# Full-height state matmuls and a layer norm moved between convolution columns, in a fused mixer and expert block on one core

## The chip, the cores and the metric

One Trainium2 chip, one of its cores. The core has a matrix engine (TensorE, PE in the profile, with PEld for its weight loads), VectorE (DVE), ScalarE (ACT), GpSimd (POOL), SyncE (SP, which only issues transfers here) and 16 DMA engines. The metric is device microseconds of one execution, lower is better. All tensors are float32 in memory.

## The reference

A transformer-like block on 2048 tokens of width 1024: an adaptive norm, a mixer of two branches, and a mixture of 64 experts. The change touches the mixer only:

```python
h = rms_norm(x, g_pre_mix[l]) * (1.0 + sc_m) + sh_m
z = h @ w_in[l]                                   # z_val | z_gate | z_ssm, 512 columns each
a_out = conv_module(z_val * jax.nn.sigmoid(z_gate), ...)   # depthwise conv of 31 taps, layer norm, silu
b_out = s5_layer(z_ssm, ...)                      # 32 groups: complex state space model, 64 states each
mixed = jnp.concatenate([rms_norm(a_out, g_out_conv[l]), rms_norm(b_out, g_out_ssm[l])], axis=-1)
o = mixed @ w_out[l]
x = x + gt_m * rms_norm(o, g_post_mix[l])

# in s5_layer
bu_r = jnp.einsum('blgh,gph->blgp', uf, bbr)      # and bu_i
_, _, s_r, s_i = lax.associative_scan(_complex_affine_combine, (lam_r, lam_i, bu_r, bu_i), axis=1)
y = (jnp.einsum('blgp,ghp->blgh', s_r, c_re) - jnp.einsum('blgp,ghp->blgh', s_i, c_im) + d_skip * uf)
g = jax.nn.gelu(y)
out = g * jax.nn.sigmoid(g @ w_glu + b_glu)
```

After the mixer come routing (8 of 64 experts for each token), the routed and the shared experts, and a last norm.

## The kernel before, in words

The 2048 tokens are worked through in two halves (`NH` = 2, index `h`) of 1024. A half goes through these stages on PE, in this order in the program:

- `z_ssm(h)`: eight units (`("zs", h, j)`), each 8 matmuls of 128x512, that give u for the state space model; then `u_transposed(h)`, 32 transposes.
- `inputs_to_state(h)`: the input of every chunk of 8 tokens to the states. Four groups `n`, each of two accumulator banks (real and imaginary, `("V", h, n, w)`), from a ring of four banks `dv`, which VectorE frees.
- `z_conv(h)`: 16 units (`("zc", h, q, b, w)`), each 8 matmuls of 128x512, that give value and gate of the convolution branch for channel block `q`; in half 0, transposes of x for half 1 stand between them (`turn_unit`).
- `outputs(h)`: for each of the 32 state groups `g` one accumulation of three matmuls of 128x128: the part inside the chunk (`TOE`, 128 rows high), the real states (`SR`, 64 rows) and the imaginary states (`SI`, 64 rows). A pair of groups shares one tile, one group in the lower and one in the upper 64 partitions. The accumulators (`("Y", h, n)`) are in the ring of two banks `mm`; ScalarE applies the gelu once a pair of banks is full.
- `g_transposed(h)` and `glu(h)`: transposes and the gate matmul.

VectorE runs, for each half, `states(h)` (four groups: phasors, a scan for each of the four pairs and both parts, phasors again) and `conv(h)` (four channel blocks, each one tensor_scalar and 30 scalar_tensor_tensor of 128x1024, accumulated in `cacc`). The layer norm of a half (`norm_turns`, eight token tiles `i`) passes all engines for each tile: PE transposes `cacc` (`("LF", h, i)`), ScalarE copies it to `ytok`, VectorE takes mean and variance (`norm_stats`), GpSimd normalises into `yn`, PE transposes back (`("LB", h, i)`), ScalarE applies gain, bias and sigmoid, GpSimd multiplies and SyncE stores from one of two slots (`bo`). There is one `ytok` and one `yn`. In half 0 the nine turns of this stand between the units of `z_ssm(1)`; in half 1 they follow the end of the GLU and the ada blocks (`ada`, matrix-vector products of the adaptive norm), three of which stand between them. `conv(1)` may overwrite `cacc` only when the last tile of half 0 has been transposed.

Then the output projection begins (`mix_half`), which needs all stored tiles; ScalarE's first square for it (L1411) stands behind its part of the last layer norm turn. Every engine takes its work strictly in the order that the program writes; the numberings `tpk`, `mmk` and `dvk` give the banks of the rings, `sgk` and `bok` the slots of the sigmoid tiles and of the stores. Waits are semaphores.

## Time and profile before

| | us |
|---|---|
| median of the three runs | 3013.49 (3012.6 to 3021.64) |
| the profiled execution, its own time | 3023.36 |
| its span | 3021.6 |
| PE busy | 2710.6 (90%) |
| VectorE busy | 1548.0 (51%) |
| GpSimd busy | 1456.6 (48%) |
| ScalarE busy | 1147.0 (38%) |
| PE's share of the chain that ended last | 61% |
| mixer, up to the first output projection matmul | 796.6 |
| output matmuls, half 0 and half 1 | 54.2 and 55.1 |
| z columns of half 1 | 110.1 |

How to read it: the span is one execution as the hardware profiler saw it. A row of a timeline gives the start, the time from start to end, the engine, the line and operation, what it writes and reads and how many, and in brackets how long the engine was idle before it and which instruction released it. Windows give for a stretch the busy time of each engine (and its instructions), the granted clock of PE as a part of 2.4 GHz, and the share and rate of the DMA engines. A float32 matmul shows as two records, a transpose as one. A busy time is an average over stages with different limits, and the mixer and the experts are limited by different things; the change is in the first quarter of the span.

### The profile page before, as it was taken

How to read it: one execution, taken by the hardware profiler on the slowest of the kernel's cores; microseconds unless marked ns; L12 is line 12 of the kernel's file. 1: busy time of each engine (PE TensorE's matmuls, PEld its weight loads, DVE VectorE, ACT ScalarE, POOL GpSimd, SP SyncE). 2: the span in 40 equal slices, each digit the busy share in tenths (PEclk: the TensorE clock that was granted, in tenths of full speed). 3: DMA queues.
4: the chain of work that ended last, by engine and by line, in shares of the span. 5: the costliest groups of instructions: out<-in, count | busy, mean ns of one | idle time of the engine just before them, and what ended most of it. 6: DMA issues, size and time to landing. Idle time of an engine off the chain costs nothing.

```text
span 3021.6 us, 49743 instructions
## 1 busy us (share of the span) xinstructions
PE 2710.6 (90%) x11527; PEld 1951.1 (65%) x11528; DVE 1548.0 (51%) x2565; ACT 1147.0 (38%) x1537; POOL 1456.6 (48%) x1756
## 2 busy tenths in 40 slices
PE   6989998999678999659999999999999999999980
PEld 2745664462345666548777777777777778777770
DVE  7389918990255666623333333443455444444525
ACT  4133231122322232124444444454555555545532
POOL 2012141112345666424455555555667767767656
PEclk8999699969779999879999999999999999999995
DMA  8152223233422232166777777778889989988977
GB/s 259 59 114 89 102 92 49 84 128 131 161 107 70 99 101 88 50 217 148 191 187 203 215 208 191 189 215 243 239 263 263 269 271 271 268 258 248 268 212 260
DMA packets 306667, 534.90 MB, mean 177 GB/s; under 512 B 40310, under 2 KB 206198, under 8 KB 305834
## 3 DMA queue, kind: packets, MB, share of 16 engines
q1 hardware_dynamic: 252826, 356.19, 35.7%
q0 software_dynamic: 51472, 173.70, 24.3%
q10 hardware_dynamic: 2304, 4.20, 0.4%
q8 instruction: 34, 0.56, 0.1%
q14 instruction: 31, 0.25, 0.0%
HBM read 396.02 MB, written 138.01 MB: 177 GB/s over the span
## 4 chain that ended last, share of the span: by engine, by line
PE 61%; issue 17%; POOL 9%; POOLq 6%; ACT 2%; DVE 2%; SPq 1%; DMA 1%; another core or an unknown queue 0%; ACTq 0%; DVEq 0%
PE psm L1111 27%; PE psm L1058 8%; PE psm L950 7%; PE psm L912 4%; PE psm L1104 2%; PE psm L851 2%; POOL arena L2147 2%; PE psm L988 2%; POOL arena L2144 2%; POOL st L2137 1%; POOLq L2143 1%; PE psm L968 1%; PE psm L967 1%; POOLq L2165 1%; PE psm L1048 1%
## 5 line engine op out<-in xcount | busy, mean ns | idle before, releaser
L1111 PE MATMUL psm<-whi,xhi 128*128 (+1 forms) x1424 | 577.6, 406 | 65.2 <-issue 33.8
L1111 PE MATMUL psm<-whi,xlo 128*128 (+1 forms) x1424 | 559.8, 393 | 0.0
L1111 PE MATMUL psm<-wlo,xhi 128*128 (+1 forms) x1424 | 558.5, 392 | 0.0
L1900 DVE TENSOR_TENSOR arena<-psm,arena 128x256 f32<-128x256 f32 x178 | 75.7, 425 | 653.2 <-ACT arena L1461 645.0
L1111 PEld LDWEIGHTS psm<-whi,xhi 128*128 128x128 f32 x1424 | 269.4, 189 | 139.3 <-issue 67.8
L2152 POOL TENSOR_TENSOR wlo<-raw,whi (+1 forms) x64 | 330.3, 5161 | 42.3 <-ACT whi L1490 42.3
L1111 PE MATMUL psm<-whi,hhi 128*128 (+1 forms) x712 | 295.4, 415 | 41.2 <-issue 19.9
L1739 DVE SCALAR_TENSOR_TENSOR arena<-arena,cw 128x1024 f32<-128x1024 f32 x240 | 326.9, 1362 | 8.6
L1111 PEld LDWEIGHTS psm<-whi,xlo 128*128 128x128 f32 x1424 | 269.5, 189 | 59.2
L2161 POOL DMA_INDIRECT acc_d<-arena x162 | 278.6, 1720 | 58.6 <-issue 54.3
L1111 PEld LDWEIGHTS psm<-wlo,xhi 128*128 128x128 f32 x1424 | 270.4, 190 | 51.7
L1916 DVE TENSOR_TENSOR wlo<-raw,whi (+1 forms) x256 | 296.5, 1220 | 2.8 <-ACT whi L1486 2.8
L1461 ACT ACTIVATE arena<-psm 128x256 f32<-128x256 f32 x178 | 68.4, 384 | 601.8 <-PE psm L1111 594.0
L1111 PE MATMUL psm<-whi,hlo 128*128 (+1 forms) x712 | 282.1, 396 | 0.0
L1111 PE MATMUL psm<-wlo,hhi 128*128 (+1 forms) x712 | 281.2, 395 | 0.0
L1467 ACT COPY arena<-psm 128x1024 f32<-128x1024 f32 x162 | 164.2, 1014 | 224.3 <-PE psm L1111 158.7
L1486 ACT CAST whi<-raw (+1 forms) x256 | 249.4, 1051 | 0.0
L1058 PE MATMUL psm<-arena 128*128 128x512 f32 x512 | 235.6, 620 | 0.0
L1896 DVE TENSOR_TENSOR xlo<-psm,xhi 128x1024 fp32r<-128x1024 f32 x163 | 199.6, 1225 | 66.0 <-ACT xhi L1457 63.5
L950 PE MATMUL psm<-arena 128*128 128x512 f32 x512 | 221.4, 593 | 0.0
L1457 ACT CAST xhi<-psm 128x1024 fp32r<-128x1024 f32 x163 | 165.7, 1017 | 83.7 <-PE psm L1104 83.2
L2147 POOL DMA_INDIRECT arena<-h_d,arena x165 | 179.5, 1088 | 37.1 <-issue 23.9
(354 smaller groups left out, 4024.6 us busy)
## 6 DMA issues: line engine op xcount, KB each, us to landing
raw<-in_we_gate_dram SPq DMA_DIRECT2D x64, 1024.0 KB
raw<-in_we_up_dram SPq DMA_DIRECT2D x64, 1024.0 KB
raw<-in_we_down_dram SPq DMA_DIRECT2D x64, 1024.0 KB
arena<-in_w_ada_dram SPq DMA_DIRECT2D x12, 2048.0 KB
arena<-in_x_dram SPq DMA_DIRECT2D x32, 512.0 KB, 6.0
h_d<-arena SPq DMA_DIRECT2D x17, 512.0 KB, 2.7
acc_d<-arena SPq DMA_DIRECT2D x17, 512.0 KB, 3.6
arena<-in_w_in_dram SPq DMA_DIRECT2D x16, 512.0 KB, 5.5
```

Of the source, the lines that this page charges most:

```text
L950: m = TE.matmul(b[:, :], wz_conv(q)[:, w, k, :], hT[:, k, b2 * 512:(b2 + 1) * 512], start=(k == 0), stop=(k == KD - 1))
L1058: m = TE.matmul(psm[:, 2 * f + c, :], mixb[:, i % 2, f * CT + q, :], wout[:, f * CT + q, c * 512:(c + 1) * 512], start=(q == 0), stop=(q = ...
L1111: m = TE.matmul(o, a, w, start=(n == 0), stop=(n == len(todo) - 1))
L1457: SC.copy(xhi[:, :], psm[:, 2:4, :].rearrange("p a n -> p (a n)")).then_inc(s_xt_high, 1)
L1467: SC.copy(yb[w], psm[:, 4:6, :].rearrange("p a n -> p (a n)")).then_inc(s_y_act, 1)
L1486: SC.copy(whi[:, bass.ds(slot + c * GC, GC)], raw[:, bass.ds(slot + c * GC, GC)]).then_inc(s_whi_ready, 1)
L1739: m = stt(o, v[:, q, k:k + HT], cw[:, q, k:k + 1], o, ALU.mult, ALU.add)
L1896: tt(xlo[:, :], psm[:, 2:4, :].rearrange("p a n -> p (a n)"), xhi[:, :], ALU.subtract).then_inc(s_xt_ready, 1)
L1916: m = tt(wlo[:, bass.ds(slot + c * GC, GC)], raw[:, bass.ds(slot + c * GC, GC)], whi[:, bass.ds(slot + c * GC, GC)], ALU.subtract)
L2147: PO.indirect_dma_start(xg[w], None, h2_d, bass.IndirectOffsetOnAxis(idxg[w], 0)).then_inc([s_xr_in0, s_xr_in1][w], 16)
L2152: PO.tensor_tensor(wlo[:, bass.ds(slot + WG, FE * D)], raw[:, bass.ds(slot + WG, FE * D)], whi[:, bass.ds(slot + WG, FE * D)], ALU.subtrac ...
L2161: PO.indirect_dma_start(acc_d, bass.IndirectOffsetOnAxis(idxs, 0), yb[w], None, compute_op=ALU.add).then_inc(s_ya_out, 16)
```

## The change

The states of a group are no longer in two tiles of 64 rows. `states` writes its last step by halves of the partitions into `SS`, in which real states are in the lower and imaginary states in the upper 64 partitions of each group, so that `outputs` multiplies `SS[:, g]` by one coefficient block `CO[:, g]` of 128 rows: two matmuls for a group, both 128 rows high, instead of three. The coefficients are built from two transposed blocks (`Y1`, `Y2`) with three operations for each of eight powers instead of six on half the width. The accumulators of the outputs come from the ring `dv` of four banks instead of `mm`.

```diff
                 for n in range(8):
-                    b = take_mm(("Y", h, n))
+                    b = take_dv(("Y", h, n))
                     pe.wait_ge(s_states_ready, 4 * h + n // 2 + 1)
                     for j in range(4):
-
-                        g = 8 * (n // 2) + 2 * j + n % 2
-                        r, lo = g // 2, (n % 2) * S
+                        g = 4 * n + j
                         o = b[:, j * P:(j + 1) * P]
                         TE.matmul(o, UT[:, g, :], TOE[:, g, :], start=True, stop=False)
-                        TE.matmul(o, SR[lo:lo + S, r, :], COR[lo:lo + S, r, :], start=False, stop=False)
-                        m = TE.matmul(o, SI[lo:lo + S, r, :], COI[lo:lo + S, r, :], start=False, stop=True)
-                    m.then_inc(s_mm_full, 1)
+                        m = TE.matmul(o, SS[:, g, :], CO[:, g, :], start=False, stop=True)
+                    m.then_inc(s_dv_full, 1)
...
-                    for w, (a, x0, x1, op) in enumerate(((SR, t[0], t[1], ALU.subtract), (SI, t[2], t[3], ALU.add))):
-                        add(tt(a[:, r, 1:NC], x0[:, :, 0:NC - 1], x1[:, :, 0:NC - 1], op))
+                    stacked = both.rearrange("p (r f c) -> p f r c", r=4, f=2)
+                    for w, (x0, x1, op) in enumerate(((t[0], t[1], ALU.subtract), (t[2], t[3], ALU.add))):
+                        for lo, hi, f in halves:
+                            o = stacked[w * S:(w + 1) * S, f]
+                            add(tt(o[:, :, 1:NC], x0[lo:hi, :, 0:NC - 1], x1[lo:hi, :, 0:NC - 1], op))
+                            if h:
+                                add(V.tensor_copy(o[:, :, 0], last[lo:hi, w, r]))
```

The input states of a half are issued in four pieces: groups 0 and 1 ahead of the columns, groups 2 and 3 behind the first and the second column unit. The layer norm of half 0 leaves `z_ssm(1)` and stands behind the first ten column units of half 1, on PE, ScalarE and GpSimd alike; a tile comes back two turns after it went out instead of one, and `ytok`, `yn` and `bn` are double.

```diff
             def z_conv(h):
                 units = list(UNITS) if h == 0 else []
...
+                for n in range(2):
+                    input_state(h, n)
+                for u, (q, b2, w) in enumerate(ZC_UNITS):
...
+                    if u < 2:
+                        input_state(h, u + 2)
...
+                    if h == 1 and u < TPH + 2:
+                        norm_turn(0, u)
...
+            def norm_turn(h, i):
+                if i == 0:
+                    pe.wait_ge(s_conv_ready, CT * (h + 1))
+                if i < TPH:
+                    b = take_tp(("LF", h, i))
+                    for q in range(CT):
+                        m = TE.transpose(b[:, q * P:(q + 1) * P], cacc[:, q, i * P:(i + 1) * P], ident[:, :])
+                    m.then_inc(s_tp_full, 1)
+                if i >= 2:
+                    b = take_tp(("LB", h, i - 2))
+                    pe.wait_ge(s_yn_ready, h * TPH + i - 1)
+                    for q in range(CT):
+                        m = TE.transpose(b[:, q * P:(q + 1) * P], yns[h][i % 2][:, q * P:(q + 1) * P], ident[:, :])
+                    m.then_inc(s_tp_full, 1)
```

On VectorE the statistics of half 0's tiles are placed inside `states(1)`; on SyncE the stores of these tiles come between the table and weight loads of half 1:

```diff
+                    if h and n >= 2:
+                        norm_stats(2 * n - 3)
...
+                    if h and 1 <= n <= 3:
+                        norm_stats(2 * n - 2)
+                if h:
+                    for k in range(5, TPH):
+                        norm_stats(k)
...
-            for i in range(TPH):
+            for i in range(2):
                 store_bo(("ln", 0, i))
             load_toe(1)
             load_wz_conv(1, 2)
+            for i in range(2, 6):
+                store_bo(("ln", 0, i))
             load_wz_conv(1, 3)
+            for i in range(6, TPH):
+                store_bo(("ln", 0, i))
```

How this stands on PE, from the end of half 0's GLU to the outputs of half 1. Before: L912 is z_ssm, L1002 and L1008 are the two transposes of a layer norm turn, L923 transposes u, L938 is the input states, L950 the columns.

```order
L912 MATMUL psm<-arena 128x512 x8
L1002 MATMUL psm<-ident,arena 128x128 x4
L1008 MATMUL psm<-ident,arena 128x128 x8
L923 MATMUL psm<-ident,arena 128x128 x32
L938 MATMUL psm<-arena 64x128 x64
L950 MATMUL psm<-arena 128x512 x128
```

And of the changed kernel, where L915 is z_ssm, L926 transposes u, L941 is the input states, L954 the columns, L1003 and L1009 the two transposes of a turn:

```order
L915 MATMUL psm<-arena 128x512 x64
L926 MATMUL psm<-ident,arena 128x128 x32
L941 MATMUL psm<-arena 64x128 x32
L954 MATMUL psm<-arena 128x512 x8
L941 MATMUL psm<-arena 64x128 x16
L1003 MATMUL psm<-ident,arena 128x128 x4
L954 MATMUL psm<-arena 128x512 x8
L941 MATMUL psm<-arena 64x128 x16
L1003 MATMUL psm<-ident,arena 128x128 x4
L954 MATMUL psm<-arena 128x512 x8
L1003 MATMUL psm<-ident,arena 128x128 x4
L1009 MATMUL psm<-ident,arena 128x128 x4
```

The eight units of z_ssm now stand in one piece, the last two input-state groups stand behind a column unit each, and the turns of the layer norm begin behind the first column unit.

On VectorE, the third of the four state groups of half 1 (L1717 is its scans, L1722 and L1723 its second phasor products, L1729 and L1731 the stacked writes and their first columns, L1737 the signal to PE, L1690 the statistics of a tile):

```order
L1717 SCALAR_TENSOR_TENSOR arena<-lam,last,arena 128x128 x8
L1690 BN_STATS bn<-arena 128x6
L1691 BN_AGGR bn<-bn 128x2
L1722 TENSOR_TENSOR arena<-arena 128x512 x2
L1723 TENSOR_TENSOR arena<-arena 128x512 x2
L1729 TENSOR_TENSOR arena<-arena 64x4x127
L1731 COPY arena<-last 64x4
L1729 TENSOR_TENSOR arena<-arena 64x4x127
```

Before, the same place held two writes of 128 partitions instead of four of 64, and the eight statistics stood in a row ahead of the first group. Now the first statistics stand behind the second group, and the last three between the fourth group and the convolution.

## Rows read from the trace of the kernel before

**Rows 1.** Windows of the mixer's stages: us, busy us of each engine, clock, DMA:
```profile
151.00:157.50 6.50, 4.60 (x33) 3.37 (x32) 0.00 (x0) 4.88 (x10) 0.00 (x0) 1.00 0.85 230
...
157.50:174.00 16.50, 8.67 (x128) 8.29 (x128) 14.84 (x33) 8.56 (x13) 3.54 (x8) 0.79 0.16 38
...
292.40:346.60 54.20, 52.14 (x194) 39.58 (x192) 52.73 (x42) 5.94 (x9) 1.39 (x3) 0.60 0.23 88
346.60:357.00 10.40, 7.96 (x33) 5.86 (x32) 10.11 (x9) 9.28 (x11) 0.00 (x0) 0.50 0.56 205
357.00:386.70 29.70, 29.67 (x64) 13.19 (x65) 19.93 (x14) 6.09 (x8) 12.70 (x21) 0.93 0.37 123
386.70:463.10 76.40, 70.11 (x225) 51.94 (x223) 7.71 (x22) 30.17 (x65) 35.49 (x51) 0.96 0.27 90
...
480.40:590.50 110.10, 110.10 (x258) 48.90 (x257) 107.41 (x119) 8.87 (x15) 12.06 (x21) 1.00 0.31 48
...
655.60:683.30 27.70, 27.68 (x65) 12.10 (x66) 27.13 (x17) 6.07 (x8) 12.88 (x21) 1.00 0.70 247
...
683.30:722.80 39.50, 39.50 (x92) 6.69 (x91) 0.39 (x1) 11.18 (x13) 2.38 (x5) 1.00 0.65 225
...
722.80:793.20 70.40, 37.65 (x119) 13.32 (x119) 10.77 (x22) 24.72 (x53) 33.72 (x46) 0.72 0.36 128
```

**Rows 2.** Timeline of PE, input states of half 0 (start, us, line, records, idle before):
```profile
157.56 5.46 PE L938 MATMUL psm<-arena 128*64 128x128 f32 x96 [0.67 <-ACT arena L1311]
...
170.79 3.32 PE L938 MATMUL psm<-arena 128*64 128x128 f32 x32 [7.77 <-DVE arena L1705]
```

**Rows 3.** Timeline of PE, output matmuls of half 0:
```profile
292.42 0.39 PE L967 MATMUL psm<-arena 128*128 128x128 f32 x2
...
292.74 0.48 PE L968 MATMUL psm<-arena 64*128 64x128 f32 x2
...
313.28 0.79 PE L967 MATMUL psm<-arena 128*128 128x128 f32 x2
...
315.91 0.80 PE L967 MATMUL psm<-arena 128*128 128x128 f32 x2 [0.69 <-ACT arena L1342]
```

**Rows 4.** Windows: transposes of x; one us in the outputs of each half:
```profile
67.00:76.00 9.00, 7.59 (x46) 4.90 (x44) 8.76 (x22) 8.31 (x13) 0.00 (x0) 0.96 0.10 41
...
303.00:304.00 1.00, 1.00 (x6) 0.77 (x5) 1.00 (x1) 0.00 (x0) 0.00 (x0) 0.65 0.99 410
...
600.00:601.00 1.00, 1.00 (x6) 0.80 (x4) 0.96 (x2) 0.11 (x1) 0.00 (x0) 0.63 1.03 422
```

**Rows 5.** Timeline of VectorE: convolution of half 0, states, convolution, layer norm:
```profile
377.21 0.18 DVE L1746 COPY arena<-arena 128x30 f32<-128x30 f32 x1
...
475.51 0.67 DVE L1704 TENSOR_TENSOR arena<-psm,arena 128x512 f32<-128x512 f32 x1
...
486.63 0.67 DVE L1704 TENSOR_TENSOR arena<-psm,arena 128x512 f32<-128x512 f32 x1
...
510.83 0.81 DVE L1737 TENSOR_SCALAR arena<-arena,cw,col 128x1024 f32<-128x1024 f32 x1
...
724.10 0.69 DVE L1754 BATCH_NORM_STATS2 bn<-ytok 128x6 f32<-128x512 f32 x1 [40.41 <-ACT ytok L1372]
```

**Rows 6.** Timeline of GpSimd, normalising a tile:
```profile
726.09 2.09 POOL L2069 TENSOR_SCALAR arena<-ytok,bn,st 128x512 f32<-128x512 f32 x1
```

**Rows 7.** Timeline of SyncE, table loads of half 1:
```profile
480.56 9.37 SPq L610 DMA_DIRECT2D arena<-kd_d  x8
```

**Rows 8.** Timeline of PE, first turn of the last layer norm, next ada block:
```profile
728.33 1.09 PE L1008 MATMUL psm<-ident,arena 128*128 128x128 f32 x4 [4.45 <-POOL arena L2069]
...
729.35 9.02 PE L851 MATMUL psm<-arena,ccol 128*1 128x512 f32 x16
```

**Rows 9.** Timelines of SyncE and GpSimd, last tiles of the last layer norm:
```profile
774.51 19.49 SPq L619 DMA_DIRECT2D mix_d<-bo  x5
...
783.56 1.26 POOL L2058 TENSOR_TENSOR bo<-ly,arena 128x512 f32<-128x512 f32 x1 [11.33 <-DMA mix_d<-bo]
```

More of the change, by code:

```diff
@@ L357, in build @@
         UNIT_STEPS = (3, 3, 2, 0, 2, 2, 2, 2)
+        ZC_UNITS = [(q, b, w) for q in range(CT) for b in range(2) for w in range(2)]
         tpk = []
@@ L889, in tables @@
                 pe.wait_ge(s_c_ready, 1)
-                for w in range(3):
+                for w in range(2):
                     b = take_dv(("C", w))
@@ new lines, in z_conv @@
+                for u, (q, b2, w) in enumerate(ZC_UNITS):
+                    if b2 == 0 and w == 0:
+                        pe.wait_ge([s_wz_in0, s_wz_in1][q % 2], (80, 64)[q % 2] * h + 32 * (q // 2 + 1))
+                    b = take_mm(("zc", h, q, b2, w))
+                    for k in range(KD):
+                        m = TE.matmul(b[:, :], wz_conv(q)[:, w, k, :], hT[:, k, b2 * 512:(b2 + 1) * 512],
+                                      start=(k == 0), stop=(k == KD - 1))
+                    m.then_inc(s_mm_full, 1)
+                    if u < 2:
+                        input_state(h, u + 2)
+                    if h == 0 and w == 1:
+                        for n in range(UNIT_STEPS[2 * q + b2]):
+                            turn_unit(1, *units.pop(0))
+                    if h == 1 and u < TPH + 2:
+                        norm_turn(0, u)
@@ L1029, in _ @@
                 ada(n)
-            norm_turns(1)
+            for i in range(TPH + 2):
+                norm_turn(1, i)
+                if 1 <= i <= 3:
+                    ada(8 + i)
             pe.wait_ge(s_mm_free, len(mmk))
@@ L1403, in _ @@
                 ada(n)
-            norm_turns(1)
+            for i in range(TPH + 2):
+                norm_turn(1, i)
+                if 1 <= i <= 3:
+                    ada(8 + i)
             def square_mix(i):
@@ L1702, in states @@
                     r = slice(4 * n, 4 * n + 4)
+                    both = us[:, n * 1024:(n + 1) * 1024]
+                    SR, SI = (both[:, w * 512:(w + 1) * 512].rearrange("p (r c) -> p r c", r=4) for w in range(2))
                     vr = got(("V", h, n, 0)).rearrange("p (r c) -> p r c", r=4)
@@ L2025, in gate @@
             def gate(h):
-                for q in range(CT):
-                    for b in range(2):
+                for u, (q, b, w) in enumerate(ZC_UNITS):
+                    if w == 1:
                         pool.wait_ge(s_mm_free, MMN["zc", h, q, b, 1] + 1)
@@ L2035, in gate @@
                             row_stats(3)
+                    if h == 1 and u < TPH + 2:
+                        norm_turn(0, u)
             def out_slot(key):
@@ L2088, in _ @@
             PO.memset(st[:, 61:62], 0.0).then_inc(s_zero_ok, 1)
-            norm(1)
+            for i in range(TPH + 2):
+                norm_turn(1, i)
             pool.wait_ge(s_row_ready, 1)
```

281 lines of the change are left out of this document (114 added, 167 removed).

## The prediction

> **What bounds the kernel now.** I read the windows by stage first, to see which engine is full where; then the timelines at the seams between stages, where an engine waits; then the way from the last layer norm into the output projection, since that is where every microsecond won before it has to arrive. The matrix engine (PE) sets the pace of the mixer. In the windows it is busy nearly all the time in the z columns (110.1 of 110.1 us), in the output matmuls (52.1 of 54.2 us in half 0) and in the GLU [rows 1], so what it no longer does there comes off. Three places are slow for other reasons. The input-state stage of half 0 takes 16.5 us for work that PE does in about 7: it waits 7.77 us for VectorE to give back accumulators, and runs the last quarter at the low clock [rows 1, 2]. The output matmuls start at 0.32 us each (292.42 to 292.74) and end at 0.65 each (three of them between 313.28 and the 0.69 us gap before 315.91) [rows 3]: the granted clock falls from 1.00 to 0.50, that is from 2.4 to 1.2 GHz, in the window 303 to 304, and its mean over the stage is 0.60 [rows 1, 4]. And half 0's layer norm stands between z_ssm of half 1 and the next stage, 76.4 us for all of it, the transposes of u included [rows 1].
>
> VectorE is the other engine that matters. The convolution of half 1 begins at 510.83; four channel blocks later, at 683.7, VectorE goes idle for 40.41 us, until PE has come to the last layer norm at 722.8 [rows 5]. So the convolution of half 1 has 39 us of slack behind PE. This slack decides what the change is worth.
>
> **The change, part by part**, on the profiled execution (span 3021.6 us, 3023.4 us with what lies around it; that is 0.3% above the median of the runs, 3013.5, so I take the difference from it and set it on the median).
>
> (a) Input states among the columns. PE does the first 96 records of this stage in 5.46 us [rows 2], so all 128 take 7.3; the third and fourth group of banks now come behind a column unit of 6.9 us each (110.1 / 16, rows 1), by when VectorE has freed the banks (it reads a group's two banks in the first four of its operations, at 0.67 us each, and needs 11.1 us for the group, rows 5). 16.5 - 7.3 = **9.2 us** off PE in half 0.
>
> (b) Output matmuls. 64 in a half instead of 96. At 0.32 us [rows 3] they take 20.5, at 0.65 us 41.6. A full-height one costs what a half-height one costs: the first row of the pair at 292.42 is full height, and the next starts 0.32 us after it. I take 20.5, since I expect the clock to stay up, for two reasons in the rows: the two thirds of matmuls that used 64 of 128 rows are gone, and the gap of 0.69 us, two banks waiting for ScalarE, goes with the ring of four banks; in both halves it fell, in the windows 303 to 304 and 600 to 601 [rows 4], a little after the first such gap, 10 to 11 us into the stage. In the stage of transposes of x from 67 to 76 us PE had more idle time than the outputs will have (7.59 of 9.0 us busy) and kept a clock of 0.96 over it, all full height [rows 4]. So 54.2 - 20.5 = **33.7 us** off half 0. If it falls after 11 us as before, 34 are done by then and 30 x 0.65 = 19.5 follow: 30.5 in all, 23.7 off.
>
> The Trainium skill, "TensorE: Matmul & The Clock Gate", section "Why this matters for your kernels", ties the loss of the fast clock to idle gaps between bursts of matmuls; by that alone the outputs would not have fallen at all, with one gap of 0.69 us, and the measured row decides against it. By the page the sum is as it stands, by the row taken alone (the outputs fell while busy, so they fall again) it is 12 us less.
>
> (c) What follows the outputs in half 0 starts at full clock: transposes 10.4 to 9.3 us (eight ScalarE copies of about 1.0 set them), GLU 29.7 to the 27.7 that half 1 has at clock 1.00 [rows 1]. **3.1 us**.
>
> (d) Layer norm of half 0 leaves the z_ssm stage. Left are eight units of 7.0 and the transposes of u, 6.5 [rows 1]: 62.7 instead of 76.4, **13.7 us**.
>
> (a) to (d) bring the input states of half 1 from 463.1 to 463.1 - 59.7 = 403.4. VectorE ends the convolution of half 0 at 377.4 before [rows 5]; its four state groups of half 0 grow by 1.3 us each, so near 382 now, and it is free by then.
>
> (e) The z columns of half 1 carry the layer norm. PE's own work: 7.3 + 110.1 + 16 x 0.44 for transposes = 124.5. But turn i asks for the normalised tile of turn i - 2, and that passes VectorE (statistics placed inside the state groups: the first only after two groups), GpSimd and ScalarE, each in order. Walking the turns through all four engines, with VectorE's group at 11.1 us [rows 5] plus 2 x 0.61 for two more stacked writes and 0.2 for copies, lengthened to 13.2 for contention, and a GpSimd pass of 3.8 (2.09 for the normalising itself [rows 6], 1.1 for the two small steps and hand-overs ahead of it, from 725.0 to 726.09, and the rest for contention), PE waits 9 us in turns 4 to 6 and does the last unit at +134. The eighth tile leaves for VectorE at +77, its copy and statistics take 1.7, and only then may the convolution overwrite its accumulator: it starts at **+79** (before: +47.7). With nothing stretched it is +76, with 15% more +83. So 403.4 + 79 = 482.4 instead of 510.8, and at the same 172.9 us its end is **655.3**. PE is there at 403.4 + 134 + 20.5 + 9.3 + 27.7 + 39.5 (five ada blocks [rows 1]) = 634.4. It waits 21 us. All that half 1's outputs save, 55.1 - 20.5 = 34.6 us, is inside this wait, and so is a weight load that now queues behind the table load (9.4 us of issue [rows 7]), which may hold PE up to 10 us at column unit 8.
>
> (f) The last layer norm starts at 655.3 instead of 722.8: **67.5 us**. It no longer waits 4.45 us for the first tile [rows 8]; against it PE comes out of the long wait at the low clock, and pays 2 us as the first ada block did before (9.02 instead of 7.0) [rows 8]. Two transposes in a row come first: 2.3 us gained. Behind the last ada block SyncE's queue sets the pace as before: the modulation is stored, the row constants are loaded, then the fourth tile is stored at 774.5, and GpSimd, which needs its slot, goes on at 783.56 [rows 9]. Then three steps instead of four, about 2 us gained. Together **4 us**, between 0 and 6.
>
> VectorE's table of output coefficients is three 512-wide operations a step instead of six 256-wide: about 2 us less, in a stretch where it is idle afterwards. Nothing for it, nor for the third coefficient transpose, behind which PE waited for ScalarE anyway. The experts stage is untouched; I take 0, within 5 either way.
>
> Sum: 67.5 + 4 = 71.5 us. 3023.4 - 71.5 = 2951.9 for the profiled run; on the median, 3013.5 - 71.5 = **2942 us**.
>
> **Rivals.**
> 1. The clock falls in the outputs all the same (for it: PE is 96% busy there and it fell; against: full height, no gap). Half 0 then gives 12 us less ((b) 10, (c) 2 to 3), and half 1's loss disappears in the wait: 2954. One variant: the Trainium skill's same page, section "Part 4: PE-mode transpose", says that transposes don't count as activity for the clock. By that only (c) would go, 2945, with a chance of 0.04 inside the forecast's range. The rows speak against it: the clock stood at 0.96 over 9 us in which PE did nothing but transposes [rows 4].
> 2. The turns of the layer norm hold each other up more than in my walk: GpSimd's products stretch while VectorE works (state groups now coincide with them). Each 5 us later at the eighth tile is 5 us on the end, to +95: 2945 to 2958.
> 3. Slower than before: the turns don't overlap at all. One turn is then a unit 6.9, transposes 0.9, copy 0.6, statistics 1.0, GpSimd 3.8 + 2.0 + 1.9 for normalising, product and gate, ScalarE 2.2 and a store of 2 that holds the output slot: 21 us, eight of them 168. The convolution starts at +172, ends at 748, and the total is 3013 + 25 - 4 = 3034. It decides from a turn of 18 us on; between 8 and 10 are in the walk, so it takes a double.
> 4. The 4 us of (f) or the experts stage move by another phase of the queues: 2936 to 2950. In the forecast's range.
>
> **How the numbers follow.** Forecast 0.60 (2935 to 2949), rival 1 0.24, rival 2 0.11, slower 0.02, other 0.03. The range 2929 to 2961 takes in the forecast, rival 1 with its spread, and most of rival 2. About 0.3% is what a measurement of this kernel can tell from no change, 9 us: no case but the serial one comes near it. Faster 0.96, same 0.02, slower 0.02.
>
> **What would show it.** After: no idle of VectorE's making in the input states of half 0; output stages near 21 us with clock 1.00 (rival 1: 30, mean near 0.7); input states of half 1 at 403; first convolution step of half 1 at 482, 79 us later; an idle time of PE near 21 us before the last layer norm, released by VectorE, where before VectorE idled 40; the first output-projection matmul at 722. The forecast is wrong if PE doesn't wait for the convolution there: then half 1's outputs count, and the sum of (e) is the step that failed.

## The result and the profile after

The changed kernel takes 2939.64 us (median of 4 runs, 2926.55 to 2954.06), the kernel before 3015.78 in the same comparison (4 runs, 3012.6 to 3021.64): a ratio of 0.976, 95% interval 0.972 to 0.980. The profiled execution took 2938.84 us, its span is 2937.1. Forecast were 2942 us, between 2929 and 2961. Against the 3015.78 us of the same comparison the gain is 76.1 us, where 71.5 were forecast; the four runs of the changed kernel lie 27.5 us apart, so the total alone can't test a sum of terms of a few microseconds. The marks below can.

The times that follow are marks in the mixer, read as starts of instructions on PE. From the start of the program to the input states of half 0 all kernels here but the one before have the same code, and yet that mark lies anywhere from 154.7 to 159.0 us; so the columns behind the first count from it. Even from there to the input states of half 1 the same code takes 238.6 to 240.3 us (six kernels), so a difference of marks under 2 us between two runs says nothing. Each experiment was executed once, but for the last two (six times); the mixer is read from one profiled execution each.

| kernel | input states of half 0 | to those of half 1 | to the last layer norm | from there to the output projection | mark to output projection | rest of the span |
|---|---|---|---|---|---|---|
| before | 157.6 | 305.5 | 565.2 | 73.8 | 639.0 | 2225.0 |
| after | 155.0 | 239.3 | 494.1 | 74.8 | 568.9 | 2213.3 |

The mixer gave 70.2 us from that mark on (72.8 with the 2.6 us ahead of it). The rest of the span, where the code is the same, was 11.7 us shorter; over the ten profiled runs of the changed kernel and of its variants with the same output that part lies between 2194 and 2220 us, so 12 us are within what it varies by, and I take them for no effect of the change.

PE's windows after, by stage: input states and the first two column units of half 0; outputs, transposes of g and GLU of half 0; z columns of half 1; outputs of half 1; five ada blocks (columns as in [rows 1]):

```profile
154.90:176.60 21.70, 21.61 (x161) 12.88 (x161) 19.82 (x42) 11.06 (x16) 4.70 (x9) 1.00 0.12 29
281.10:295.40 14.30, 14.30 (x130) 14.30 (x129) 13.94 (x12) 5.94 (x9) 2.30 (x3) 1.00 0.75 284
295.40:305.10 9.70, 6.16 (x34) 4.22 (x32) 9.45 (x8) 9.17 (x11) 0.00 (x0) 0.82 0.78 290
305.10:332.70 27.60, 27.58 (x65) 12.40 (x66) 26.99 (x18) 6.08 (x8) 14.93 (x21) 1.00 0.39 133
394.30:538.60 144.30, 128.94 (x448) 63.20 (x449) 125.44 (x170) 29.90 (x63) 55.16 (x69) 0.95 0.31 51
538.60:553.00 14.40, 14.40 (x130) 14.39 (x129) 14.04 (x11) 5.14 (x8) 2.27 (x3) 1.00 0.81 292
589.60:629.20 39.60, 39.57 (x91) 6.69 (x90) 38.60 (x30) 11.18 (x13) 2.46 (x7) 1.00 0.65 225
```

The outputs take 14.3 and 14.4 us in the two halves at clock 1.00, where [rows 1] has 54.2 at 0.60. The next rows are PE's timeline: the input states, now 3.71 and twice 1.97 us with no wait for VectorE (against 7.77 us in [rows 2]), a wait for a weight load at the ninth column unit of half 1, the wait for the convolution, and the output projection.

```profile
154.99 3.71 PE L941 MATMUL psm<-arena 128*64 128x128 f32 x64 [0.68 <-ACT arena L1306]
165.70 1.97 PE L941 MATMUL psm<-arena 128*64 128x128 f32 x32
174.66 1.97 PE L941 MATMUL psm<-arena 128*64 128x128 f32 x32
...
481.14 1.22 PE L954 MATMUL psm<-arena 128*128 128x512 f32 x1 [9.81 <-DMA arena<-in_w_in_dram]
...
649.07 1.97 PE L1003 MATMUL psm<-ident,arena 128*128 128x128 f32 x8 [19.90 <-DVE arena L1754]
...
720.44 3.54 PE L1046 MATMUL psm<-one,arena 128*128 128x1 f32 x16 [21.34 <-ACT arena L1403]
723.84 2.06 PE L1056 MATMUL psm<-arena 128*128 128x512 f32 x2
```

Before the last layer norm it is now PE that waits, 19.90 us, for the last operation of the convolution (L1754), where VectorE waited 40.41 [rows 5]. VectorE's timeline: it is done with the convolution of half 0 at 382, waits 12.71 us for half 1's input states, then idles in the layer norm's last statistics before the convolution of half 1 (L1752) starts at 472.42.

```profile
382.06 0.42 DVE L1698 TENSOR_TENSOR arena<-lam,last 128x16 f32<-128x16 f32 x4
395.49 0.69 DVE L1706 TENSOR_TENSOR arena<-psm,arena 128x512 f32<-128x512 f32 x1 [12.71 <-PE psm L941]
...
464.53 0.69 DVE L1690 BATCH_NORM_STATS2 bn<-ytok 128x6 f32<-128x512 f32 x1 [7.35 <-ACT ytok L1366]
471.60 0.69 DVE L1690 BATCH_NORM_STATS2 bn<-arena 128x6 f32<-128x512 f32 x1 [6.15 <-ACT arena L1366]
472.42 0.80 DVE L1752 TENSOR_SCALAR arena<-arena,cw,col 128x1024 f32<-128x1024 f32 x1
```

### The profile page after: what moved, and what is told of

Read it like the earlier page. It is cut to its first block, busy times and chain, and to the rows that moved or that the text cites. A ratio compares the mean times of both kernels' runs of the same rounds, so it can differ in the third digit from the quotient of the medians.

```text
span 2937.1 us, 49464 instructions
## 1 busy us (share of the span) xinstructions
PE 2620.7 (89%) x11395; PEld 1888.8 (64%) x11396; DVE 1571.1 (53%) x2558; ACT 1145.9 (39%) x1534; POOL 1471.7 (50%) x1756
## 4 chain that ended last, share of the span: by engine, by line
PE 51%; issue 19%; POOL 11%; DVE 9%; POOLq 7%; ACT 2%; DMA 1%; SPq 1%; DVEq 0%; ACTq 0%
PE psm L1109 25%; PE psm L1056 8%; DVE arena L1754 6%; PE psm L954 5%; PE psm L915 4%; POOL arena L2149 3%; POOL arena L2146 2%; PE psm L1102 2%; POOL st L2139 2%; POOLq L2145 2%; POOLq L2167 2%; PE psm L854 1%; PE psm L1046 1%; POOLq L2166 1%; POOLq L2158 1%
## 5 line engine op out<-in xcount | busy, mean ns | idle before, releaser
L1754 DVE SCALAR_TENSOR_TENSOR arena<-arena,cw 128x1024 f32<-128x1024 f32 x240 | 335.7, 1399 | 8.6
L954 PE MATMUL psm<-arena 128*128 128x512 f32 x512 | 226.5, 600 | 9.8 <-DMA arena<-in_w_in_dram 9.8
L1911 DVE TENSOR_TENSOR hlo<-psm,hhi 128x256 fp32r<-128x256 f32 x178 | 74.9, 421 | 230.0 <-ACT hhi L1471 228.1
```

The source lines that it names most:

```text
L954: m = TE.matmul(b[:, :], wz_conv(q)[:, w, k, :], hT[:, k, b2 * 512:(b2 + 1) * 512], start=(k == 0), stop=(k == KD - 1))
L1754: m = stt(o, v[:, q, k:k + HT], cw[:, q, k:k + 1], o, ALU.mult, ALU.add)
```

## Experiments

A line in a diff is against the changed kernel. Where a kernel's output differs, the experts stage routes other tokens, so only the mixer is read there. "Relative" means against the mark of the input states of half 0.

### What the output matmuls cost, and what let the clock fall

**Two 64-row matmuls for the second one.**

```
+ lo = (n % 2) * S
- TE.matmul(o, SS[:, g, :], CO[:, g, :], start=False, stop=True)
+ TE.matmul(o, SS[lo:lo + S, g, :], CO[lo:lo + S, g, :], start=False, stop=False)
+ TE.matmul(o, SS[lo:lo + S, g, :], CO[lo:lo + S, g, :], start=False, stop=True)
```

> The changed kernel, but its second output matmul of 128 rows is replaced by two of 64 rows on the same 64 rows (rows 0 to 63 in even banks, 64 to 127 in odd ones, as the kernel before alternated), 96 matmuls in a half; half of the state is left out and the other half counted twice, so its output is not the reference's. The ring of four banks stays, so no bank waits for ScalarE. If the height of the rows sets the pace: 0.35 us each as at the start of the stage before (1.06 us for three), 34 us for the stage of half 0 instead of 14.4. If only the number counts: 96 x 0.225 = 21.6. If the fall of the clock before came from the ScalarE gap of 0.69 us, the clock stays at 1.00 in this stage; if it comes from the half-height matmuls, it falls to 0.50 some 11 us into the stage and the stage takes about 50 us. Half 0's growth shows in full at the first output projection matmul (723.8 in the changed kernel): 731 by the count alone, 743 by the height with the clock up, 760 to 764 with the fall. Half 1's growth disappears in PE's wait of 19.9 us before the last layer norm as long as it is under that.

Measured: 33.8 us in both halves, clock 1.00 all through (PE's windows over the outputs, the last of half 1; then a group of three on PE's timeline, L973 of 128 rows, L975 and L976 of 64, and the first of the next group):

```profile
282.80:293.00 10.20, 10.20 (x61) 7.90 (x60) 9.95 (x8) 3.71 (x5) 2.28 (x3) 1.00 0.64 224
293.00:304.00 11.00, 11.00 (x64) 8.46 (x63) 10.71 (x10) 1.08 (x2) 0.00 (x0) 1.00 0.56 224
304.00:316.50 12.50, 12.50 (x73) 9.60 (x72) 12.14 (x11) 1.09 (x2) 0.00 (x0) 1.00 0.00 0
560.50:594.30 33.80, 33.80 (x194) 26.02 (x193) 32.94 (x26) 5.14 (x8) 1.39 (x3) 1.00 0.33 125
```

```profile
283.71 0.49 PE L973 MATMUL psm<-arena 128*128 128x128 f32 x2
284.13 0.48 PE L975 MATMUL psm<-arena 64*128 64x128 f32 x2
284.46 0.38 PE L976 MATMUL psm<-arena 64*128 64x128 f32 x2
284.77 0.49 PE L973 MATMUL psm<-arena 128*128 128x128 f32 x2
```

33.8 / 96 = 0.352 us each against 14.4 / 64 = 0.225. The count alone would have given 21.6. Half 1's growth of 19.4 us used up PE's wait, and relative the output projection came 21.3 us later (absolute 746.8, expected 743).

**Only 64-row matmuls.** The same, and:

```
- TE.matmul(o, UT[:, g, :], TOE[:, g, :], start=True, stop=False)
+ TE.matmul(o, UT[lo:lo + S, g, :], TOE[lo:lo + S, g, :], start=True, stop=False)
```

> As the run with two 64-row matmuls, but all three matmuls of a group use 64 rows, so none is of full height and the height changes nowhere inside a bank; half of the inner sum is left out, the output is not the reference's. If 64 rows in themselves are slow: 0.32 us each (as the second and third record of a group before), 31 us in half 0. If the alternation of 128 and 64 rows is what costs: 0.225 each, 21.6 us. Clock: at 0.50 after about 11 us if half-height matmuls let it fall, and then the stage takes 40 us or more; 1.00 all through if the ScalarE gap was the cause.

Measured:

```profile
284.00:303.30 19.30, 19.30 (x194) 19.18 (x194) 18.80 (x16) 5.79 (x9) 2.21 (x3) 1.00 0.65 246
```

19.3 / 96 = 0.201 us each. That mean is again a mixture. On PE's timeline, inside a bank and where the next bank begins:

```profile
284.51 0.38 PE L976 MATMUL psm<-arena 64*128 64x128 f32 x2
284.73 0.38 PE L974 MATMUL psm<-arena 64*128 64x128 f32 x2
...
286.30 0.27 PE L975 MATMUL psm<-arena 64*128 64x128 f32 x1
286.30 0.37 PE L974 MATMUL psm<-arena 64*128 64x128 f32 x1
```

Inside a bank a matmul comes every 0.22 us, as at full height. Where a bank on rows 0 to 63 is followed by one on rows 64 to 127, records of both start at the same time and overlap for a few matmuls; that lowers the mean. So 64 rows in themselves are not slow; it is the change between 128 and 64 rows. A group of three with it takes 1.056 us; three at 0.223 would be 0.67, so each of its two changes costs about 0.19 us. The Trainium skill, "TensorEngine Tiling (Array Packing)", section "Key Properties", says that a change of the tiling mode drains the matrix engine. The cost at each change of height fits that; the drain itself is in no trace here.

**The ring of two banks, all matmuls at full height.** With it go the waits and ScalarE's reads:

```
- b = take_dv(("Y", h, n))
+ b = take_mm(("Y", h, n))
```

> The changed kernel with its output matmuls (two of full height a group, as in the changed kernel) writing the ring of two banks again that they shared with the z columns before; nothing else is undone. It measures the other part of the change to the outputs. PE fills a bank in 1.8 us and ScalarE empties one in about 1.0, but begins only when both banks of a pair are full, so PE should wait some 1.5 to 2 us at each of the three seams between pairs: stage of half 0 at 19 to 21 us instead of 14.4. Theory A (the fall of the clock before was the gaps' doing: it fell about 1 us after the first ScalarE gap, and with mixed heights and no gaps it did not fall): the clock falls to 0.50 here too in the stage or in the transposes behind it, and the stage takes 24 us or more. Theory B (it takes the stage's longer duration or the half-height matmuls as well): the clock stays at 1.00 and the stage is 19 to 21 us. In half 0 the growth shows in full at the last layer norm, 654 to 660 with the input states at 155.0; in half 1 it disappears in PE's wait.

Measured: 17.3 us in either half, clock 1.00, with three waits for ScalarE:

```profile
288.55 0.49 PE L973 MATMUL psm<-arena 128*128 128x128 f32 x2 [0.69 <-ACT arena L1339]
293.08 0.49 PE L973 MATMUL psm<-arena 128*128 128x128 f32 x2 [0.69 <-ACT arena L1339]
297.60 0.49 PE L973 MATMUL psm<-arena 128*128 128x128 f32 x2 [0.69 <-ACT arena L1339]
```

The ring of four is worth 2.9 us by itself. The expectation was too high: ScalarE works beside PE, and the wait is 0.69, not 1.5 to 2. In both halves of this execution the gaps alone didn't bring the clock down.

**Both edits at once.**

> The changed kernel with both of the earlier edits at once: the 64-row pairs (second and third matmul of a group on the same 64 rows, half of the state left out and the other counted twice, so the output is not the reference's, and the experts stage routes other tokens: only the time up to the output projection is compared) and the ring of two banks. Each alone left the clock at 1.00 through the stage (33.8 and 17.3 us). Theory (it takes both, the mixed heights and a gap of 0.69 us at ScalarE): the clock falls to 0.50 some 11 us into the stage of each half, as before, and the stage takes 50 to 55 us. Rival (the fall depends on what lies ahead of the stage, such as the four groups of input states in one piece or the banks' phase, and not on the output matmuls): clock 1.00, 34 + 2 = 36 us.

Measured: 55.7 and 53.7 us (before: 54.2 and 55.1). PE's windows up to the first gap (which ends at 291.89) and behind it:

```profile
282.80:291.20 8.40, 8.40 (x50) 6.39 (x48) 8.22 (x6) 2.64 (x3) 2.30 (x3) 1.00 0.57 190
291.80:303.00 11.20, 11.11 (x36) 8.55 (x36) 10.88 (x11) 0.52 (x2) 0.00 (x0) 0.51 0.64 258
303.00:338.40 35.40, 34.03 (x110) 25.69 (x109) 34.43 (x29) 2.17 (x4) 0.00 (x0) 0.50 0.00 1
```

The granted clock falls behind the first gap of 0.69 us and stays at 1.2 GHz to the end of the stage. In half 0 it falls at once; in half 1, where the gap ends at 593.13, some 2.5 us later; in the kernel before, 1.8 and 0.6 us behind it. So in the output stage the fall took both, the mixed heights (or the slower pace that they bring) and the gap; either alone left 2.4 GHz in both halves of its execution.

The DMA engines moved 400 to 430 GB/s at each of these falls; they did so for some 8 us in each of the two runs with one edit as well, so that alone isn't it. The fall isn't a fixed answer to a gap either: in the changed kernel the clock fell at 300 us, in the transposes of g of half 0, all of full height, after a gap of 1.37 us, and in half 1 it didn't after one of 1.38. Why is open.

The Trainium skill, "TensorE: Matmul & The Clock Gate", section "Why this matters for your kernels", which the prediction weighed, ties a loss of the fast clock to idle gaps of PE. The runs agree in that the mixed stage kept its clock without a gap; but here a gap was not enough, three of 0.69 us left it up at full height.

### Where the saved time counts

**Output matmuls of one half done twice**, in half 1, then (`h == 0`) in half 0.

```
+ for again in range(2 if h == 1 else 1):
      TE.matmul(o, UT[:, g, :], TOE[:, g, :], start=True, stop=False)
      m = TE.matmul(o, SS[:, g, :], CO[:, g, :], start=False, stop=True)
```

> The changed kernel, with each pair of output matmuls of half 1 done twice (the second time it starts the sum again), 128 of full height instead of 64; nothing else. Theory of the slack: the stage of half 1 takes 28.8 us instead of 14.4, PE's wait for VectorE before the last layer norm shrinks from 19.9 to 5.5 us, and the last layer norm starts at 649 as before: the first output projection matmul stays at 724 within 1.5. Rival (PE counts there): it comes 14 us later, at 738. A second thing to see: 0.225 us a matmul and clock 1.00 over 28.8 us, if it is height and not the short stage that kept the clock up.

> The same doubling in half 0 alone: stage 28.8 us instead of 14.4. Theory: half 0's PE time counts in full, input states of half 1 at 408.7 instead of 394.3, last layer norm at 663.5 instead of 649.1, first output projection matmul at 738.2 instead of 723.8. Rival (something else, VectorE's convolution of half 0 or a load, holds half 1 back, so that half 0's saving was in part hidden): less than 10 us later.

Measured: stage 28.8 us in the half that is doubled, clock 1.00. The row that PE starts the last layer norm with, for half 1 doubled and for half 0 doubled:

```profile
649.06 1.97 PE L1004 MATMUL psm<-ident,arena 128*128 128x128 f32 x8 [6.46 <-DVE arena L1755]
```

```profile
666.55 1.75 PE L1004 MATMUL psm<-ident,arena 128*128 128x128 f32 x7 [19.37 <-DVE arena L1755]
```

14.4 us more in half 1 moved the output projection by 0.6 us (relative 569.4 against 568.9): they came out of the wait, 19.90 to 6.46. In half 0 the relative marks moved by 13.6 (input states of half 1), 13.7 (last layer norm) and 13.9 us (projection), and the wait stayed. The missing 0.7 us are the transposes of g, whose clock didn't fall there.

**All input states ahead of the columns.**

```
- for n in range(2):
+ for n in range(4):
      input_state(h, n)
...
- if u < 2: input_state(h, u + 2)
```

> The changed kernel, but all four groups of input states stand ahead of the z columns again, in both halves. Theory: in half 0 PE waits for VectorE's banks as before, 16.5 us instead of 7.3 of work, +9.2 on the input states of half 1 (403.5). In half 1 it costs PE the same 9.2, but PE idles 5.5 us in turns 2 to 4 of half 0's layer norm for VectorE, which is not delayed; so the convolution of half 1 starts 3.7 later after the input states (81.8 instead of 78.1), and the last layer norm and the first output projection matmul come 12.9 later: 662 and 737. Rival (the last group was slow by the low clock alone, and no wait returns): under 5 us in all.

Measured: the stage of half 0 takes 18.7 us, with this wait:

```profile
172.80 3.68 PE L941 MATMUL psm<-arena 128*64 128x128 f32 x32 [9.54 <-DVE arena L1705]
```

Relative, the input states of half 1 come 11.5 us later and the last layer norm 16.0. The shape is as expected (half 1 adds 4.5, expected 3.7); the size of half 0 is not: the wait that returns is 9.54, not the 7.77 of [rows 2]. The trace has the 1.77 us: VectorE's first group lasts 12.47 us here (its first reads start at 159.01, those of the second group at 171.48) and 10.70 before (158.77 and 169.47). With the stacked writes a group is longer, and a bank comes free later by as much.

**Half 0's layer norm back in z_ssm of half 1.** PE, ScalarE:

```
  for h in range(NH):
+     for i in range(CH + 2 if h else 0):
+         if i < CH: z_ssm(1, [i])
+         norm_turn(0, i)
```

and the turns leave `z_conv` and `gate`, the statistics go back between `conv(0)` and `states(1)`.

> The changed kernel with stacked states and its two-turns-deep layer norm, but half 0's layer norm is back between the eight units of z_ssm of half 1, and VectorE's statistics between its convolution of half 0 and the states of half 1. The output work is unchanged. Theory: z_ssm of half 1 starts at 333, the first turn must wait for the convolution of half 0, which ends at 382, some 42 us; then seven more units with turns at 7.9 each, two turns of 4 and 6.5 of u transposes bring the input states of half 1 to about 453 instead of 394; the convolution of half 1 starts some 53 later, near 506 instead of 472, and the last layer norm at 680 instead of 649: +31 us in the total, 2970. That is, of the 72 us the stacking gives 41 alone and the move of the layer norm 31 on top. Rival (the layer norm's place is worth only its own PE time, 13.7 us): 2952 or less.

Measured: PE stands in the first turn until VectorE has done the convolution of half 0,

```profile
382.36 1.11 PE L998 MATMUL psm<-ident,arena 128*128 128x128 f32 x4 [41.42 <-DVE arena L1750]
```

and the relative marks are 302.1 (+62.8), 530.2 for the last layer norm (+36.1) and 605.4 for the projection (+36.5, expected 31). So of the 70.2 us in the mixer this kernel, whose turns are still two deep, has 33.6, and the move gives 36.5 on top. Without it, most of what half 0 saves ahead of the convolution's end would be waited away at 382.

### The stretch behind the convolution

**SyncE's order.** Modulation stores ahead of tile stores, the zero stores ahead of the wait for the modulation (left out below), tiles 2 and 3 around the router weights' load:

```
  for n in range(9, 12):
+     store_mod(n)
+     if n < 11: store_bo(("ln", 1, n - 9))
-     store_bo(("ln", 1, n - 9))
-     store_mod(n)
...
+ store_bo(("ln", 1, 2))
  SY.dma_start(wr, ...)
+ store_bo(("ln", 1, 3))
  SY.dma_start(rbias, ...)
```

> The changed kernel with another order in SyncE's queue behind the last layer norm: each modulation store ahead of the layer norm tile that becomes ready after it, the zero stores ahead of tile 2's store, tile 2 after the row loads, tile 3 ahead of the 4.3 us issue of the router bias instead of behind it and four more loads. Theory (SyncE's order lost the forecast's 4 us behind the last ada block): row loads at 683 instead of 691.6, tile 3 stored at 691 instead of 702.7, GpSimd's product of tile 5 no longer waits 14.0 us, and the first output projection matmul comes 8 us earlier, between 4 and 12, at 716. The last layer norm's start (649) doesn't move. Rival (the loads' landing, 8 to 10 us each with the DMA engines busy, sets it anyway): within 2 us of 724.

In the changed kernel, SyncE's queue and GpSimd's product of tile 5 look so:

```profile
685.92 0.28 SPq L553 DMA_DIRECT2D mod_d<-arena  x1
...
691.59 1.75 SPq L700 DMA_DIRECT2D arena<-mod_d  x4
...
696.06 4.32 SPq L702 DMA_DIRECT2D arena<-in_b_router_dram  x1
...
702.69 1.01 SPq L618 DMA_DIRECT2D mix_d<-bo  x2
...
711.90 1.26 POOL L2073 TENSOR_TENSOR bo<-ly,arena 128x512 f32<-128x512 f32 x1 [14.04 <-DMA mix_d<-bo]
```

Measured with the other order (SyncE, then GpSimd):

```profile
687.14 1.75 SPq L700 DMA_DIRECT2D arena<-mod_d  x4
...
693.56 4.12 SPq L618 DMA_DIRECT2D mix_d<-bo  x1
...
702.11 1.62 POOL L2075 TENSOR_TENSOR bo<-ly,arena 128x512 f32<-128x512 f32 x1 [5.42 <-DMA mix_d<-bo]
```

From the last layer norm to the projection 66.4 us instead of 74.8: 8.3 less, expected 8; from the mark 561.5 instead of 568.9, 7.4 less. GpSimd still waits 5.42 us. The slow issue of some 4 us is not the router bias's own: here tile 3's store, which now stands in that place, took 4.12 us, and the bias behind it 0.76.

**Turns closer together.** Turns 5, 6 and 7 of half 0's layer norm behind column unit 5.

> The changed kernel with turns 5, 6 and 7 of half 0's layer norm all behind column unit 5, and 8 and 9 behind units 6 and 7; elsewhere the same. Theory: VectorE idles 13.5 us before turns 6 and 7 because a column unit of 6.9 us stands between them, though the states are done; without the units a turn takes the 4 us or so of its chain through four engines, so the convolution of half 1 starts 6 us earlier (466 instead of 472), the last layer norm at 643 instead of 649, and all after it 6 us earlier; PE's wait before it shrinks from 19.9 to 10 to 14. Rival (the chain of a turn is nearly as long as a unit, or GpSimd's gate of the z columns comes late and holds the convolution): under 2 us.

Measured: the convolution of half 1 starts 75.2 us after its input states instead of 78.1. VectorE's waits before it:

```profile
465.31 0.69 DVE L1691 BATCH_NORM_STATS2 bn<-ytok 128x6 f32<-128x512 f32 x1 [6.85 <-ACT ytok L1367]
...
469.89 0.69 DVE L1691 BATCH_NORM_STATS2 bn<-arena 128x6 f32<-128x512 f32 x1 [3.67 <-ACT arena L1367]
```

Half of what was expected. The first of the two waits hardly shrank: ScalarE's part of turn 6 stands behind the gain of tile 3, that behind GpSimd's gate product of unit 5, and that behind the normalising of tile 4. The first turn without a unit took 7.8 us, longer than a column unit, the second 4.6. PE's wait before the last layer norm fell to 10.73 us, but what counts came hardly earlier: relative, the last layer norm 1.9 us and the projection 1.3 us (6 were expected), which is within what the marks vary by. So a gain for the mixer as a whole is not shown.

**The ada blocks ahead of the last layer norm.**

```
- for n in range(NADA, 9):
+ for n in range(NADA, 12):
      ada(n)
  for i in range(TPH + 2):
      norm_turn(1, i)
-     if 1 <= i <= 3: ada(8 + i)
```

and in SyncE's program the stores of tiles 0 to 2 move behind the loads, to the other five.

> A version that spends PE's wait of 19.9 us before the last layer norm: the ada blocks 9, 10 and 11, which stood inside the layer norm's turns 1 to 3, run ahead of its first turn, behind blocks 4 to 8; so in SyncE's queue the modulation stores, the row constants, the router weights and the first loads of the output projection go ahead of all tile stores. Theory (the wait is real slack, and behind the last layer norm the ada blocks and SyncE's order set the pace): PE ends block 11 at 629.2 + 3 x 7.9 = 653, 4 us after the convolution, so the layer norm starts at 653 instead of 649; its eight tiles then run at the 4.6 us a turn that turns 4 to 7 show, the first output projection matmul comes about 47 us later, at 700 instead of 724, and the total falls by 24 us, between 15 and 30, to 2915; against the kernel before 0.967. Rival (the loads' landing, 8 MB with the DMA engines full, or the loads of blocks 9 to 11, hold PE or the first projection): less than 10 us gained.

**The same with SyncE's queue put in order.**

```
  store_mod(8)
+ # zero stores, loads of rtmp[:, 0..2], load_xs(0), load_xs(1)
  for n in range(9, 12): store_mod(n)
+ # loads of wr, rbias; wait for the modulation stores; loads of row[0..3]
...
  for i in range(2): load_mix(i)
  for i in range(TPH): store_bo(("ln", 1, i))
```

> The version with the ada blocks ahead of the last layer norm, and SyncE's queue ordered by when things are ready: the zero stores, the three row constants that don't depend on the modulation, and the first two x tiles ahead of the modulation stores 9 to 11; the router weights and bias while the last modulation store lands; then the four modulation rows, two loads for the projection and the tile stores. Theory (in the version with the blocks ahead, GpSimd waited 6.2 us and ScalarE 8.2 for output slots, because tile 0, ready at 667, was stored at 671.6 behind the 4.4 us issue of the router bias and landed with the DMA engines full): the waits for the slots go, tile 7's product ends near 697, the first output projection matmul comes 8 us earlier, 701 instead of 708.8 (with input states at 155.3), and the total is 2910, between 2905 and 2914. Rival (the chain of a turn through four engines, 4.6 us, sets it already): under 3 us gained.

Measured, PE with the blocks ahead, then with the queue in order as well:

```profile
654.02 1.09 PE L1002 MATMUL psm<-ident,arena 128*128 128x128 f32 x8
...
708.81 2.05 PE L1053 MATMUL psm<-arena 128*128 128x512 f32 x2
```

```profile
654.52 1.09 PE L1003 MATMUL psm<-ident,arena 128*128 128x128 f32 x8
...
703.00 2.06 PE L1054 MATMUL psm<-arena 128*128 128x512 f32 x2
```

PE has no wait left before the layer norm, and from there to the projection it is 54.8 and 48.5 us instead of 74.8. From the mark to the projection: 553.5 and 546.1 instead of 568.9, 15.4 and 22.8 us less. For the first 24 were expected: it still waited for output slots, 6.2 us on GpSimd at tile 3. The first version changes two things, the blocks' place and the place of the tile stores; what the blocks' place gives by itself was not run, and a change of SyncE's order alone was worth 7.4 us above. For the second 701 - 155.3 = 545.7 was expected. The totals: 2917.99 us (6 runs, 2915.05 to 2930.77), ratio to before 0.970 (0.967 to 0.973), and 2917.14 (2912.34 to 2937.74), 0.969 (0.966 to 0.973). The first median is 22 us under the changed kernel's 2939.64, but its own comparison had a lower median for the kernel before, 3010.99; by the ratios it is some 17 us, and their intervals overlap by 0.0005. Between the two versions the total shows no difference (2910 was expected): the 7.4 us of the mixer are less than what the experts stage varies by, so that step is shown in the mixer's trace alone.

## Why the prediction was right, point by point

The total came within 2.4 us. The mechanism held up to the last layer norm, but the sum owes its closeness in part to luck. From the first mark to the output projection 71.5 us were forecast and 70.2 measured; (a) to (d) gave 66.2 instead of 59.7, the convolution began 0.9 earlier behind them and lasted 3.7 longer, and (f) lost 1.0 where 4 were to be gained: 6.5 + 0.9 - 3.7 - 5.0 = -1.3. The rest of the total, 2.6 us ahead of the mark and 11.7 behind the mixer in the profiled pair, comes from no term of the prediction.

- **What bounds the kernel, and the slack of half 1.** Right. PE's pace carries through in half 0 (13.7 us of 14.3) and not in half 1 (0.6 of 14.4). PE waits 19.90 us before the last layer norm, forecast 21, and the convolution of half 1 starts 78.1 us after the input states, forecast 79.
- **(a)** Right. No idle of VectorE's making. Between the two kernels it is 16.5 - 7.65 = 8.9 us, forecast 9.2. In the changed kernel the place among the columns is worth 11.5, since the wait that it covers would be longer by now.
- **(b)** The term that was mis-sized: 20.5 us forecast, 14.4 measured. The sentence "a full-height one costs what a half-height one costs" is true, 0.22 us each in a stage of one height; the step that failed is the price, read as 0.32 us: the distance from the first record to the second already held a change of height. The row was from a mixed stage, and every distance in it was one of that stage; the reliable figure would have been one from a stage of one height. Of the two reasons for the clock either alone would have done, and the change took away both causes. 6.1 us more than forecast arrived through half 0.
- **(c), (d)** 27.6 for the GLU as forecast. The transposes of g took 9.7 at a mean clock of 0.82, against 9.3; with the clock up they took 9.0 (half 0 doubled). z_ssm with the transposes of u took 61.6, forecast 62.7.
- **(e)** The input states of half 1 started at 394.3, forecast 403.4: 6.1 from (b), 2.6 from ahead of the first mark, the rest small. VectorE was free at 382.0. The convolution then lasted until 649.0, that is 176.6 us, where the forecast kept the 172.9 of before: 3.7 lost. It had no term for work beside the convolution. Its four channel blocks of 30 operations took 45.8, 41.4, 46.7 and 39.6 us with 20.5, 4.2, 15.9 and 0 us of GpSimd work beside them, before 42.1, 42.3, 39.6 and 45.8 with 5.6, 5.3, 0 and 12.9: in the first block GpSimd now does the end of half 0's layer norm. That fits, and no run took it apart. The weight load that queues behind the table load held PE 9.81 us, forecast up to 10, and the wait for the convolution took it in.
- **(f)** This term failed: 4 us gained were forecast, 1.0 was lost (74.8 against 73.8). The last ada block was done 29.6 us after the start instead of 34.3: 4.7 gained, where the prediction had 2.3, since it charged 2 us for the low clock that the kernel before paid too (its first block took 9.02 us, now 8.99). Behind that block 5.7 us were lost, 45.2 against 39.5, where 2 were to be gained: with the turns two deep, tile 2 is ready for its store one turn later, and SyncE's program still had this store ahead of the modulation's. The modulation was ready at 679.4 and stored at 685.92; all loads behind it, and tile 3's store behind them, came late. The step that failed took SyncE's queue for the pace "as before", without walking what the deeper turns do to the order in it. The run with the other order gives 7.4 to 8.3 us back.
- **Experts part.** Taken at 0 within 5. It was 11.7 shorter, and it varies by 26 us between profiled runs of the same code there, so the range for it, and that of rival 4 (2936 to 2950), was too narrow: a total inside it is luck as far as this part goes.
- **Rival 1** (the clock falls all the same) did not happen in the outputs. Against its variant with the transposes the trace of before says more than the prediction took from it: from 62.19 us on PE did only transposes, and in the window 67 to 68 the clock rose from 0.50 to 1.00. **Rival 2** (the turns hold each other up) did not happen: 78.1 us to the convolution, walked at 79. **Rival 3** (turns that don't overlap): in the turns in which PE waited it needed up to 10.5 us for one, column unit included (the rival decides from 18). Had the layer norm not been moved, 36.5 us of the gain would have gone, which the prediction had not priced apart.

## What to carry to other kernels

A distance between matmuls read in a stage of mixed heights is a price of the mixture: before it is used for a stage of one height, look for a stage of one height. When a change makes a pipeline deeper, walk through the queues of the engines that only issue transfers too: a store that is due a turn later and stands ahead of something that isn't holds all that follows. And when the wait at a seam has changed sides, look at once for work behind the seam that could run in it: here three blocks that had stood inside the layer norm, with the tile stores moved behind the loads, gave 15 us more.

## What the runs showed of the hardware that was not expected

- fp32 matmuls of 128x128 came every 0.22 us at full height and every 0.22 us when all had the same 64 rows, but every 0.352 us in groups of one with 128 and two with 64 rows, all at 2.4 GHz: about 0.19 us for each change. Where 64 rows were followed by the other 64, records of both overlapped, and the mean of the stage fell to 0.201 us.
- The granted clock fell to 1.2 GHz in the mixed stage with PE 96% busy, 0 to 2.5 us behind the first gap of 0.69 us (four falls, in two kernels), while 33.8 us of the same matmuls without gap, and 17.3 us of full-height ones with three such gaps, kept 2.4 GHz. Why it takes both is open.
- Behind 3.75 MB of loads for the row constants and the router weights, the next issue held SyncE's queue for some 4 us, whichever it was: the router bias, 32 KB spread over 128 partitions, took 4.32 us there; in the run with the other order tile 3's store took 4.12 in its place and the bias 0.76. In the run with the queue in order the bias took 0.58 us.
